# The last attention's heads interleaved on TensorE with its projections and the output's products

## The reference

```python
h = rmsnorm(x, norm_gains[0]) * (1.0 + sc1) + sh1
proj = h @ w_in                     # 1024 x 2304: qa, ka, va (8 heads each), qb (8), kb, vb (2 each)
out_a = softmax(qa @ ka.T * dh**-0.5 + bias_a, causal) @ va          # heads 0 to 7
out_b = softmax(qb @ kb.T * dh**-0.5 + bias_b, window 128, sink) @ vb  # heads 8 to 15
y = concatenate([out_a, out_b]) @ w_out                              # 1024 x 1024
x = x + g1 * rmsnorm(y, norm_gains[1])
```

## Time and profile before

| | |
|---|---|
| runs | 1274.74 us median of 3 (1272.74 to 1276.42) |
| profiled execution | 1275.74 us, span 1273.8 us |
| TensorE | busy 1167.5 us, 92% of the span |
| DVE, ACT, POOL | 749.5, 523.8, 120.8 us |
| granted TensorE clock, mean | 0.909 |
| chain that ended last | 84% TensorE, 8% DVE, 4% ACT, 2% issue, 1% SP queue |
| HBM | 188.38 MB read, 151 GB/s over the span |

### The profile page before, as it was taken

The page is one execution under the profiler, slowest core; times in us unless marked ns, Lnnn a source line. Parts: engine busy times, 40 slices in busy tenths (PEclk is TensorE's granted clock), DMA queues, the critical chain, the costliest instruction groups (busy, mean ns, idle before and its releaser), DMA issues.

```text
span 1273.8 us, 17497 instructions
## 1 busy us (share of the span) xinstructions
PE 1167.5 (92%) x7196; PEld 1014.8 (80%) x7196; DVE 749.5 (59%) x1126; ACT 523.8 (41%) x742; POOL 120.8 (9%) x115
## 2 busy tenths in 40 slices
PE   5989799997799999798898899999599996999997
PEld 5788699886699998676666899988496565999885
DVE  3485685446676665656775776574743445666433
ACT  4443322114354443334673543433444444655331
POOL 0005263320300000210001200000100000000000
PEclk9899899858799999897999799999898568999999
DMA  9244000014488768333673687777162003555550
GB/s 290 83 143 171 1 2 1 1 33 135 150 278 264 250 238 295 110 132 137 122 200 100 218 262 247 249 281 247 51 207 91 1 21 112 184 181 198 198 165 33
DMA packets 112271, 193.69 MB, mean 152 GB/s; under 512 B 4514, under 2 KB 84913, under 8 KB 112066
## 3 DMA queue, kind: packets, MB, share of 16 engines
q1 hardware_dynamic: 108530, 179.65, 42.4%
q0 software_dynamic: 3248, 11.83, 4.2%
q10 hardware_dynamic: 416, 1.11, 0.2%
HBM read 188.38 MB, written 4.19 MB: 151 GB/s over the span
## 4 chain that ended last, share of the span: by engine, by line
PE 84%; DVE 8%; ACT 4%; issue 2%; SPq 1%; DMA 0%; POOL 0%; ACTq 0%; DVEq 0%
PE ps L399 21%; PE ps L400 21%; PE ps L401 21%; PE ps L1864 3%; PE ps L1847 3%; PE ps L1091 2%; PE ps L1839 2%; PE ps L1102 2%; DVE XL L532 1%; PE ps L1109 1%; PE ps L1328 1%; DVE AR L1064 1%; DVE ARR L383 1%; DVE STAT L549 1%; PE ps L1283 1%
## 5 line engine op out<-in xcount | busy, mean ns | idle before, releaser
L383 DVE TENSOR_TENSOR ARR<-ring,ARR 128x2048 fp32r<-128x2048 f32 (+1 forms) x147 | 329.3, 2246 | 233.1 <-ACT ARR L372 233.1
L399 PE MATMUL ps<-XH,ARR 128*128 128x256 f32 x1232 | 355.1, 288 | 20.4 <-DVE XL L532 14.6
L372 ACT ACTIVATE ARR<-ring 128x2048 fp32r<-128x2048 f32 (+1 forms) x147 | 274.7, 1876 | 224.8 <-PE ps L401 169.8
L400 PE MATMUL ps<-XL,ARR 128*128 128x256 f32 x1232 | 352.5, 286 | 0.0
L401 PE MATMUL ps<-XH,ARR 128*128 128x256 f32 x1232 | 352.3, 286 | 0.0
L399 PEld LDWEIGHTS ps<-XH,ARR 128*128 128x128 f32 x1232 | 239.0, 194 | 24.2 <-issue 17.8
L400 PEld LDWEIGHTS ps<-XL,ARR 128*128 128x128 f32 x1232 | 239.1, 194 | 0.0
L401 PEld LDWEIGHTS ps<-XH,ARR 128*128 128x128 f32 x1232 | 238.9, 194 | 0.0
L399 PE MATMUL ps<-ARR 128*128 128x512 f32 x388 | 157.7, 406 | 10.0 <-DVE ARR L484 6.8
L400 PE MATMUL ps<-ARR 128*128 128x512 f32 x388 | 155.8, 402 | 0.0
L401 PE MATMUL ps<-ARR 128*128 128x512 f32 x388 | 155.6, 401 | 0.0
(11 more groups left out here) (333 smaller groups left out, 1401.7 us busy)
## 6 DMA issues: line engine op xcount, KB each, us to landing
ring<-in_ffn_w_gate_up_dram SPq DMA_DIRECT2D x44, 1024.0 KB, 5.7
ring<-in_w_dram SPq DMA_DIRECT2D x32, 1024.0 KB, 5.2
ring<-in_w_ada_dram SPq DMA_DIRECT2D x24, 1024.0 KB, 5.3
ring<-in_ffn_w_down_dram SPq DMA_DIRECT2D x22, 1024.0 KB, 5.0
ring<-in_even_w_in_dram SPq DMA_DIRECT2D x13, 1024.0 KB, 6.0
ring<-in_w_in_dram SPq DMA_DIRECT2D x9, 1024.0 KB, 5.3
ring<-in_mla_w_q_b_dram SPq DMA_DIRECT2D x6, 768.0 KB, 4.5
ring<-in_even_w_out_dram SPq DMA_DIRECT2D x4, 1024.0 KB, 4.7
```

What stands on the lines that cost most here:

```text
L372: e.activation(split(i)[0], raw(i), ACT.Copy).then_inc(*up("hi", ("hi", i)))
L383: e.tensor_tensor(lo, raw(i), hi.bitcast(F32), ALU.subtract).then_inc(*up("lo", ("lo", i), ("raw free", i)))
L399: e.matmul(out, lhs[0], rhs[0], start=first, stop=False)
L400: e.matmul(out, lhs[0], rhs[1], start=False, stop=False)
```

## The change

The stage is written out anew as one interleaved order. The value rows go first, then projection blocks in the order queries and keys of heads 0 to 3, 4 to 7, then kb/vb, then the queries of heads 8 to 11 and 12 to 15 (`BLOCKS_2`). Blocks 0, 2 and half of 4 stand ahead of the attention loop. Inside the loop `along` is called after the scores of each iteration: `pe_beside_items` makes a quarter of a block (12 matmuls) in iterations 0 to 17, then one output `mm3` of a finished group of heads in each iteration from 18 to 33, and two in each from 34 to 37. The last eight output `mm3` come after the loop. `act_beside_items` and `dve_beside_items` copy blocks and split pieces at fixed iterations; ACT's and DVE's own `along` stands ahead of their iteration's work. PSUM banks are fixed by hand (`banks.put`): scores in 2 and 3 and turned probabilities in 0 and 1 up to iteration 16, then one bank each (1 and 0); projections in 4 and 5; output in 3, 2, 4, 5. The attention's result goes to new buffers OT2 and no longer into XT, which the projections still read. After the loop ACT and DVE split through w1's second piece before `act_gated` and `dve_gated`; before, they split w1's first piece there.

```diff
+        BLOCKS_2 = [0, 1, 4, 5, 2, 3, 6, 7, 12, 13, 8, 9, 10, 11]
+        COLS_2 = [(128 * i if i < 8 else 512 + 128 * i, 128) for i in BLOCKS_2]
...
+        plan_rows("va2", W2, 8, 1024, 512)
         plan_columns("in2", W2, 8, COLS_2)
-        plan_rows("va2", W2, 8, 1024, 512)
...
-        def pe_attend(e, A):
+        def pe_attend(e, A, along=None):
...
-                    b = bank(e, (A.tag, "turn", i - 5))
+                    b = bank(e, (A.tag, "turn", i - 5), A.turn_at(i))
...
-                    b = bank(e, (A.tag, "score", i))
+                    b = bank(e, (A.tag, "score", i), A.score_at(i))
...
+                if along:
+                    along(e, i)
                 if 0 <= i - 6 < n:
...
+        def pe_in2_quarter(e, i, part):
+            w, use = place_of["in2", i], ("in2", i)
+            hilo = split(w)
+            if part == 0:
+                bank(e, use, 4 + (i // 2) % 2)
+                e.wait_ge(*at(("lo", w)))
+            h, c0 = part // 2, 4 * (part % 2)
+            for c in range(c0, c0 + 4):
+                k = mm3(e, ps(use)[:, 256 * h:256 * h + 256], cut(hilo, ALL, c, slice(h * P, h * P + P)),
+                        cut(XT, ALL, c), c == 0, c == 7)
+            if part == 3:
+                k.then_inc(*up("products", ("used", w), ("full", use)))
...
         def pe_in2(e):
-            pe_columns(e, "in2", 14, XT, xt_step("m0"))
...
             pe_rows(e, "va2", 8, 512, XT, xt_step("m0"))
+            for i in (0, 2):
+                for part in range(4):
+                    pe_in2_quarter(e, i, part)
+            for part in range(2):
+                pe_in2_quarter(e, 4, part)
...
+        def pe_out2(e, k0, t, j, c):
+            use, w = ("out2", t, j), place_of["out2", k0]
+            if k0 + c == 0:
+                bank(e, use, OUT_BANK[t, j])
+            if (t, j, c) == (0, 0, 0):
+                e.wait_ge(*at(("lo", w)))
+                e.wait_ge(*at(("swa", "att", k0 // 2)))
+            k = mm3(e, ps(use), cut(OT2, ALL, k0 + c, slice(t * P, t * P + P)),
+                    cut(split(w), ALL, c, slice(512 * j, 512 * j + 512)), k0 + c == 0, k0 + c == 7)
...
+        def pe_beside_items(e, i):
+            if i < 18:
+                pe_in2_quarter(e, 4 + 2 * ((i + 2) // 4), (i + 2) % 4)
+            elif i < 34:
+                n = (i - 18) % 8
+                pe_out2(e, 2 * ((i - 18) // 8), n // 4, n // 2 % 2, n % 2)
+            elif i < 38:
+                for c in range(2):
+                    pe_out2(e, 4, (i - 34) // 2, i % 2, c)
+            if i == 11:
...
+        def pe_out2_rest(e):
+            for t in range(2):
+                for j in range(2):
+                    for c in range(2):
+                        pe_out2(e, 6, t, j, c)
...
+        def act_beside_items(e, i):
+            if i in (2, 6, 10, 14, 18):
+                act_block(e, 3 + i // 2)
+                act_split(e, place_of["in2", 9 + i // 2] if i < 8 else place_of["out2", (i - 10) // 2])
...
+            elif i == 26:
+                act_split(e, place_of["out2", 6])
...
+        def dve_beside_items(e, i):
+            if i in (3, 7, 11, 15, 19):
+                dve_split(e, place_of["in2", 9 + i // 2] if i < 8 else place_of["out2", (i - 11) // 2])
+            elif i == 27:
+                dve_split(e, place_of["out2", 6])
...
+                        [PR_2[:, i] for i in range(6)], PX_2, ST_2, SNK, ["bias", "sinks"], OT2,
+                        turn_at=lambda i: i % 2 if i < 17 else 0, score_at=lambda i: 2 + i % 2 if i < 17 else 1)
...
-            pe_attend(e, SWA)
-            pe_rows(e, "out2", 8, 1024, XT, lambda c: ("swa", "att", c))
+            pe_attend(e, SWA, pe_beside_items)
+            pe_out2_rest(e)
...
-            act_attend(e, SWA)
-            split_rest(act_split, e, "out2", 8, 2)
+            act_attend(e, SWA, act_beside_items)
+            act_split(e, place_of["w1", 2])
             act_gated(e, "out2", 0)
```

More of the change, by code:

```diff
@@ L179, in take, with put @@
         return before
+    def put(self, use, i):
+        before = self.held.get(i)
+        self.held[i], self.place[use] = use, i
+        return before
     def of(self, use):
@@ L389, in sp_piece, with bank @@
             e.dma_start(raw(i), pieces[i][0]).then_inc(*up(f"ring{i % NRAW}", ("raw", i), by=16))
-        def bank(e, use):
-            before = banks.take(use)
+        def bank(e, use, i=None):
+            before = banks.take(use) if i is None else banks.put(use, i)
             if before is not None:
@@ L1853, in pe_attend @@
                     if (t, h % 4) == (0, 0):
[L1854 to L1858, removed]
+                        bank(e, (A.tag, "o", g), 6 + g % 2)
                     o = 256 * ((h % 4) // 2) + P * t
@@ L2085, in act_in2 @@
-        def act_in2(e):
[L2086 to L2098, removed]
-            e.activation(KBT[:, 1, :], ps("swap")[:, 0:256], ACT.Copy).then_inc(*up("q2", "swapped", ("free", "swap")))
-            e.wait_ge(*at(("full", "vb")))
-            e.activation(VA[:, :, 512:640], ps("vb")[:, 0:256].rearrange("p (t n) -> p t n", t=2), ACT.Copy).then_inc(
-                *up("q2", "vb", ("free", "vb")))
-            for k0 in range(0, 8, 4):
-                act_split(e, ahead("va2", k0, k0 < 4))
+        OT2 = halves(carve.off, 8, 256)
@@ new lines, in pe_beside_items @@
+        def pe_beside_items(e, i):
[8 more added lines that the diff above has]
+            if i == 11:
+                b = bank(e, "kvb", 4)
+                e.wait_ge(*at(("q2", 12)))
+                e.matmul(b[:, 0:256], cst("swap"), KBT[:, 0, :], start=True, stop=True)
+                for t in range(2):
+                    k = e.transpose(b[:, 256 + t * P:256 + t * P + P], VBT[:, t * P:t * P + P], ident)
+                k.then_inc(*up("gates", ("full", "kvb")))
@@ L2105, in act_in2 @@
+        def act_in2(e):
+            act_split(e, place_of["in2", 0])
+            act_split(e, place_of["in2", 2])
             for t in range(2):
@@ L2362, in program @@
                    "n2": ("used", place_of["mout", 6]), "m0": ("used", place_of[("gu", 1, 20, 1), 0]),
[L2363 removed]
+                   "m1": ("used", place_of["in2", 12])}
         for reading in (tensor, scalar, vector, gpsimd, sync):
```

69 lines of the change are left out of this document (45 added, 24 removed).

## The result

Runs after: median 1254.61 us (1250.88 to 1256.06, 4 runs), before on the same chips 1273.74 (4 runs): ratio 0.9845, 95% interval 0.9814 to 0.9875. That is 19 us less where 28 were forecast. The profiled execution took 1256.06 us, its span 1254.2 us (19.6 less than before).

A forecast was written before the change was run, and what follows sets the result against it. TensorE, 92% busy, was taken to bound the kernel, its last attention at half clock. Its stretch would fall from 147.4 to 117.5 us, 29.9 less; minus 2.1 lost in the tail, 27.8 gained: 1247 us, range 1238 to 1260.

The forecast's parts named there:

- The clock: Last attention, 70.27 us, nearly all at 1.2 GHz: costs twice what it must; the change would hold 2.4 GHz.
- The joints: Every iteration: one more change between small fp32 matmuls and split products, 0.1 x 38 = 3.8 us, bounds 0 and 0.2 each.
- C and D: Loop iterations 5 to 17 with projection quarters, 32.9 us, and 18 to 31 with output groups, 25.0 us.
- A: Ahead of the loop: value rows, blocks 0, 2 and half of 4, with a 1.15 us stall: 26.7 us.
- B: Items 0 to 4: only scores and a projection quarter each, 9.1 us.
- late splits: Iterations 19 and 27: TensorE waits for DVE, delayed by a split, some 1.3 and 0.7 us, 2.0 together.
- E: Iterations 32 to 37: no scores; turnings, weighings and ten output groups, 10.8 us.
- F: Last two output chunks: 1.4 us wait for the last heads' split, eight groups and a drain, 7.2 us.
- G: Tail after the loop: X updated 1.85 us behind the products, before 0.2 ahead; 2.1 us lost.
- Rival 1: Clock falls in iterations 18 to 37, 1284 us, chance 0.08; low over the whole loop some 1325, chance 0.03.
- Rival 2: Loop bound by the score-DVE round trip on one bank or ACT's in-order queue: 1257 us, chance 0.15.
- Rival 3: Split order stalls the stage ahead of the loop, or pieces come late from the ring: 1250 to 1253, chance 0.06.

The follow-up runs named there:

- e1: Kernel before, with 14 products that nobody reads laid over the gap in the last attention's fill, nothing interleaved: 1247.29 us, ratio 0.9794.
- f5: Kernel before, with the second half of the value rows moved behind the scores of item 4: 1242.44 us, ratio 0.9751.
- e3: Changed kernel with scores made from all 128 rows, two heads at once, output not the reference's: 1244.06 us, ratio 0.9772.
- e5: g1 with the quarter or output group ahead of the score of each iteration: 1249.10 us, ratio 0.9802.
- h2: g1 with each head's keys stored in 128 rows, the other head's rows zero: 1236.15 us, ratio 0.9705.
- g1: Changed kernel with only waits moved: four output groups kept behind the loop, splits halved or shifted, another bank for the first block: 1248.23 us, ratio 0.9785.
- e2: Changed kernel with the quarter or output group ahead of the score of its iteration, not behind it: 1266.45 us, ratio 0.9916.
- e4: Changed kernel with weighings made with 128 value columns of two heads, output not the reference's: 1250.45 us, ratio 0.9824.
- h4: h2 with values padded by zeros to 128 columns as well, both heads of a pair summed in one PSUM region: 1234.25 us, ratio 0.9680.

## Why the prediction came out as it did

Faster was right, 1254.6 lies in the range, and the size was off by 7.6 us. The span that the forecast's own terms left, 1240 to 1254, did not hold it: the size of an item had no bound there. (The upper bounds as given add up to 1256.6, not 1254.) Step by step:

- **The clock**, the reason for the gain: right, and shown by e1 and f5 to be all of it. That a gap in the fill is what brings it down is shown by e1, which lays dense products over the gap and changes nothing else. "Twice what it must" was too much: a pair takes 4.56 us for 2.61.
- **The joints: the term that failed.** "I take 0.1 x 38 = 3.8 us", with 0.2 as upper bound, and 1.085 per item from the other attention. Measured: 0.70 of joints an iteration, of which the item has 0.49 (1.305 by e1, against 0.28 in the 1.085) and the interleaving adds 0.20 (2.20 less 1.305 less 0.70; a quarter, 1.61 for 1.42, gives the same 0.19). The item was 0.22 too small, which no bound allowed for, and the joint 0.1, at the upper bound: 0.315 an iteration in C and D, 27 x 0.315 = 8.5 us. A and B add 1.4 and 0.9, and late splits give 1.0 back: the 9.8. The other attention was the wrong nearest row: it has 96 rows per score, not 64, a shape that stands in the row itself. And the earlier trace rows held a better number: 4.56 us at half clock less twice the streaming of two items (2 x 1.62 = 3.24) leaves 1.32, 0.66 an item: far over 0.28, and less than twice the 0.49 of the full clock. So here the joints did not stretch with the clock as streaming does.
- **A**, 26.7: measured 28.07. The clock fell to 0.50 at 917.9, 1.1 us behind a wait of 1.98 us for the input, and was back at 921.2, so eight products took 1.5 us more. The first projection block waited 0.69 us for ACT's copy of the value rows out of its bank, a bank that the hand-made order had fixed. The wait of 1.15 us for the second piece did not come, by luck: the slow products filled its time. In e3, e5 and h2, where the clock was 1.00 there, it came with 0.97.
- **B**, 9.1 and 0.5 of joints: 10.47. **E**, 10.8 and 0.6: 11.67. **F**, 7.2: 7.3, with a wait of 1.50 for 1.4. F was right, B and E missed by joints alone.
- **Late splits**, 2.0 us: about 1.0 (waits of 0.35 and 0.57), at the iterations named. But it was ACT's copies behind ACT's split that came late, not DVE's reading.
- **G**, 2.1 us lost in the tail: 1.7. Right; g1 gives it back.
- **Account**: the stretch 20.1 shorter, X late by 1.7, and TensorE starts the stage 1.2 us earlier (916.83 for 918.07), which is not the change's doing: the turning of the input already starts at 911.56 for 912.80, ahead of every changed instruction. Together 19.6 of span.
- **Rival 1**: not in the changed kernel's loop, but e2 shows in six of ten executions that it is one stall of some 2 us away. The turnings are no danger in these loops, against the rule that the prediction weighed: 1.00 was granted throughout e1's loop, where nothing but items runs. **Rival 2**: half of it; no score waited for DVE, while ACT's order is behind every stall of the loop. **Rival 3**: 1.4 us in A, by the clock and the bank; ACT never waited for the ring.

## What to carry to other kernels

Before a stage is rewritten to save the clock, close the one gap that brings it down: five lines (e1), or one move of work that has to be done anyhow (f5), gave more than the interleaving. When small matmuls are laid between others, count the joints by shape: fill all 128 rows and columns, with zeros if need be, before interleaving. Take the cost of a joint from a row with the same rows and columns, and subtract the streamed columns from it.

## What the runs showed of the hardware

A step between matmuls on 64 rows or columns and such on 128 costs 0.10 to 0.21 us at 1.00 of the clock (and 0.11 more from the first to the second product behind a score), and the load of its weights is then not started ahead of it; full rows or columns remove nearly all of it (e3, e4), and zeros do for them (h4).

The granted clock went to 0.50 at the end of waits of TensorE or up to 2.3 us later, for waits of 2.13 and 1.66 us (e2), 2.07 (the gap in the kernel before) and 1.98 (the start of the changed kernel's stage); it stayed at 1.00 behind 1.50 and 1.28. These are single cases and no bound, since four of e2's ten executions have the mean clock of one that did not fall. Once down, it came back in e2's loop, with products between the items, after some 14 us; in the kernel before, where the items run alone, it stayed at 0.50 until the output's products, though the same items hold 1.00 when they start with it (e1).

In h4, four regions of sums are open in one PSUM bank with one start flag, set on the first matmul there, as the Trainium skill, "PSUM — Partial Sum Buffer", The four PSUM rules, has it for groups open at once in disjoint columns; the run agrees, since h4's sums come out right. What it costs in time is not measured apart.
